# Stacked fp32r scores, slabs and stores dealt out over the rounds, the scan behind the maximum, and ScalarE copying the turned weights of every unit

## What is computed

```python
h = rms_norm(x, g_pre_mix) * (1 + scale_a) + shift_a          # mod = silu(c) @ w_ada + b_ada
q, k, v, xl, yl, ga, gr = split(h @ w_in)
q, k = rope(q, pos), rope(k, pos)
# prompt: blocks of 128 queries against their own and the previous 128 keys
s = (q @ k.T) / 8;  s = where(0 <= d <= 128 and k_pos >= 0, s, -1e30)
m = maximum(max(s), sink);  p = exp(s - m)
o = (p / (sum(p) + exp(sink - m))) @ v
xc = causal_conv4(xl);  r, i = sigmoid(xc @ w_a + b_a), sigmoid(xc @ w_x + b_x)
hl = scan(a = exp(-8 r softplus(-lam)), u = sqrt(1 - a^2) * i * xc)
o_lru = hl * gelu(yl)
merged = sigmoid(ga) * (o @ w_attn) + sigmoid(gr) * (o_lru @ w_lru)
x = x + gate_a * rms_norm(merged @ w_out, g_post_mix)
# then a top-1 group, top-2 expert SwiGLU layer over 32 experts, with its own norms and modulation
```

## Time and profile before

| | us |
|---|---|
| median of 3 runs | 1672.56 (1672.17 to 1677.83) |
| the profiled execution | 1672.81, its span 1671.0 |
| TensorE busy | 1593.2 (95%) |
| VectorE / ScalarE / GpSimd busy | 744.5 / 626.4 / 126.8 |
| granted TensorE clock, mean | 0.981 |
| mean DMA rate | 242 GB/s |

### The profile page before, as it was taken

How to read it: one execution, slowest core, us unless ns; L and a number is a source line. 1 busy time by engine, 2 the same in 40 slices (tenths; PEclk the granted TensorE clock), 3 DMA queues, 4 the chain that set the end, 5 groups by cost and what they waited for, 6 DMA issues and landing times. The chain is left out here.

```text
span 1671.0 us, 27190 instructions
## 1 busy us (share of the span) xinstructions
PE 1593.2 (95%) x11089; PEld 1154.4 (69%) x11089; DVE 744.5 (45%) x1474; ACT 626.4 (37%) x1130; POOL 126.8 (8%) x218
## 2 busy tenths in 40 slices
PE   6999989999999989999999999988998999999997
PEld 2889967888888889999999989752333333333334
DVE  3523467888888764454455456660000000000006
ACT  4535545666666553343544354411110111111113
POOL 0000011111111000000000030000000000000002
PEclk7999999999999999999999999999999999999999
DMA  9464571111111385373447554979999999999988
GB/s 360 168 209 139 171 253 36 55 55 55 55 48 49 124 283 175 126 277 127 159 144 239 189 200 153 350 296 397 421 408 427 425 415 426 409 412 390 407 334 321
DMA packets 98866, 404.66 MB, mean 242 GB/s; under 512 B 13431, under 2 KB 42135, under 8 KB 85800
## 3 DMA queue, kind: packets, MB, share of 16 engines
q1 hardware_dynamic: 88816, 381.28, 59.9%
q0 software_dynamic: 6992, 17.78, 2.7%
q10 hardware_dynamic: 2936, 3.88, 0.8%
HBM read 364.83 MB, written 44.32 MB: 245 GB/s over the span
## 5 line engine op out<-in xcount | busy, mean ns | idle before, releaser
L1234 ACT ACTIVATE wup<-wraw 128x1024 fp32r<-128x1024 f32 x120 | 126.7, 1059 | 265.6 <-PE ps L2113 222.6
L1734 DVE TENSOR_TENSOR wlow<-wraw,wup 128x1024 fp32r<-128x1024 f32 x112 | 136.9, 1224 | 148.6 <-ACT wup L1234 148.0
L2113 PE MATMUL ps<-wg,xT 128*32 128x512 f32 (+2 forms) x1072 | 158.8, 621 | 11.1 <-DMA wg<-w_gate 10.3
L2113 PE MATMUL ps<-wd,aT 128*32 128x512 f32 (+2 forms) x1072 | 150.0, 596 | 6.2 <-DMA wd<-w_down 4.6
L2113 PE MATMUL ps<-wu,xT 128*32 128x512 f32 (+2 forms) x1072 | 148.6, 594 | 2.8 <-DMA wu<-w_up 2.8
L2113 PE MATMUL ps<-h_up,wup 128*128 128x384 f32 (+1 forms) x384 | 125.7, 327 | 3.4 <-DVE wlow L1734 3.4
L2113 PE MATMUL ps<-h_up,wlow 128*128 128x384 f32 (+1 forms) x384 | 124.5, 324 | 0.0
L2113 PE MATMUL ps<-h_low,wup 128*128 128x384 f32 (+1 forms) x384 | 124.5, 324 | 0.0
L2113 PEld LDWEIGHTS ps<-wd,aT 128*32 128x32 f32 (+2 forms) x1072 | 47.3, 117 | 105.6 <-issue 103.9
L2113 PEld LDWEIGHTS ps<-wg,xT 128*32 128x32 f32 (+2 forms) x1072 | 45.0, 120 | 107.5 <-issue 104.2
L2113 PE MATMUL ps<-hp_up,wA_up 128*128 128x352 f32 x312 | 107.6, 345 | 1.1 <-DVE hp_low L1488 1.1
(11 more groups left out here) (416 smaller groups left out, 3227.7 us busy)
## 6 DMA issues: line engine op xcount, KB each, us to landing
wg<-w_gate SPq DMA_DIRECT2D x32, 2048.0 KB
wu<-w_up SPq DMA_DIRECT2D x32, 2048.0 KB, 15.6
wd<-w_down SPq DMA_DIRECT2D x32, 2048.0 KB, 13.7
wraw<-w_ga SPq DMA_DIRECT2D x24, 512.0 KB, 3.7
wraw<-w_gr SPq DMA_DIRECT2D x24, 512.0 KB, 3.8
wraw<-w_at SPq DMA_DIRECT2D x24, 512.0 KB, 3.5
wraw<-w_lr SPq DMA_DIRECT2D x24, 512.0 KB, 3.5
wraw<-w_out SPq DMA_DIRECT2D x24, 512.0 KB, 3.5
```

The source lines that it names most:

```text
L1234: act.activation(wup[n % UP][:, :, :], wraw[n % RAW][:, :, :], ACT.Copy).then_inc(w_rounded, 1)
L1734: V.tensor_tensor(low_part(n)[:, :, :], wraw[n % RAW][:, :, :], wup[n % UP][:, :, :].bitcast(F32), ALU.subtract).then_inc(w_split, 1)
L2113: return pe.matmul(out, lhsT, rhs, start=start, stop=stop, skip_group_check=True)
```

## The change

1. **Scores.** Queries and keys are rounded and split after the rotation (ScalarE `round_query`, VectorE `split_query`, the same for two key tiles), stored to `q_dram` and `k_dram` with the rounded and the rest part above each other on the partitions, and loaded back for each block (`load_keys`: four DMAs of 64 partitions, `load_queries`: two a round). The contraction now holds the two parts of a query in 64 + 64 rows. Four fp32r matmuls a unit (two for each of its two heads) replace two fp32 matmuls. GpSimd has no part in the rounds any more.
2. **Round 0** takes only the second half of the keys in all steps (`c0 = P`), and the mask has no block dimension any more.
3. **Slabs**: one in step 3 of each round, two buffers; bank 1. The second modulation part is finished in round 7. Half outputs move to earlier steps.
4. **Stores**: h is stored in the rounds, one k a round; attention outputs go to a buffer of their own, `oS`, which must be stored before the next round's first output is written.
5. **The scan** stands in step 4 behind `first`, and in that step `conv` stands behind `second`.
6. **ScalarE** copies the turned weights of all units.

In the diff and in the lists below `kst` is the stacked keys and `ps<-ident,pp` a turning.

```diff
-            return (((0, 0),), ((0, 1), (1, 0)), ((1, 1), (2, 0)), ((2, 1),), ((3, 0),), ((3, 1),), ((4, 0), (4, 1)), ((5, 0), (5, 1)),
+            return (((0, 0), (0, 1)), ((1, 0), (1, 1)), ((2, 0), (2, 1)), ((3, 0),), ((3, 1), (4, 0)), ((4, 1),), ((5, 0),), ((5, 1),),
                     ((6, 1), (7, 1), (8, 1)), ((9, 1), (10, 1), (11, 1)))[s]
...
+            def q_store(u):
+
+                sp.wait_ge(kq_split, u + 3)
+                sp.wait_ge(st_kq, kq_stored(u))
+                for part in range(2):
+                    for a in range(2):
+                        sp.dma_start(head_rows(q_dram, part)[:, u, a, :], head_rows(q_part(u, part), a)).then_inc(st_kq, 16)
+
...
+            def load_keys(i):
+
+                if i < BLKS:
+                    ge(sp, u_scores, KC * (i - 1))
+                    c0 = P if i == 0 else 0
+                    for half in range(2):
+                        for a in range(2):
+                            sp.dma_start(head_rows(kst[i % 2], half)[:, a, :, c0:2 * P].bitcast(F32),
+                                         head_rows(k_dram, a)[:, :, (i - 1) * P + c0:(i + 1) * P]).then_inc(ld_kq[i % 2], 16)
...
+            sp.wait_ge(s_dve, 6)
+            sp.wait_ge(st_kq, kq_stored(KC - 1))
+            load_keys(0)
+            load_queries(0)
+            q_store(KC - 1)
+            sp.wait_ge(st_side, 64)
             for p in range(2):
-                sp.dma_start(O["kws"][:, p], kcx[:, p, :, NT:P + NT]).then_inc(st_kws, 16)
...
+                sp.dma_start(O["kws"][:, p], kcx[:, p, :, NT:P + NT]).then_inc(st_side, 16)
+            sp.wait_ge(st_kq, kq_stored(KC))
+            load_queries(1)
+            slab_halves(0)
...
             for i in range(1, KC):
                 lg_weights(i)
+                load_queries(2 * i + 1)
+                load_keys(i + 1)
+                load_queries(2 * i + 2)
+                slab_halves(i)
+                h_store(i - 1)
+                if i + 1 == KC:
+                    h_store(i)
                 o_store(i - 1)
...
-                    if 1 <= s <= KC and s % 2 == 0:
+                    if 1 <= s <= KC:
+                        w = (s - 1) % 2
                         act.wait_ge(u_turned, 8 * i + s - 1 + 3)
                         act.wait_ge(u_pv, 8 * i + s - 1 + 1)
-                        act.activation(pT[:, 1, :, :], ps[:, 6, :].rearrange("p (k q) -> p k q", k=4), ACT.Copy).then_inc(u_kept_a, 1)
+                        act.activation(pT[:, w, :, c0 // P:, :], ps[:, 5 + w, :].rearrange("p (a k q) -> p a k q", a=2, k=2)[:, :, c0 // P:, :],
+                                       ACT.Copy).then_inc((u_kept, u_kept_a)[w], 1)
                     if s >= 2:
                         act.wait_ge(u_pv, 8 * i + s - 2 + 3)
-                        act.activation(oT[:, s - 2, bass.ds(i * P, P)], ps[:, 7, 0:P], ACT.Copy).then_inc(u_out, 1)
+                        if s == 2:
+                            act.wait_ge(st_o, 16 * (i + 1))
+                            act.wait_ge(st_kq, kq_stored(KC))
+                        act.activation(oS[:, s - 2, :], ps[:, 7, 0:P], ACT.Copy).then_inc(u_out, 1)
...
             dve.wait_ge(s_pe, 8)
+            dve.wait_ge(st_kq, kq_stored(KC))
...
+                    if not begin and s == 4:
+                        lru_step(i, "scan")
+                    if 4 < s < KC or begin and s == 4:
                         conv(i, s)
                     if s < KC:
                         second(i, s)
+                    if not begin and s == 4:
+                        conv(i, s)
...
-                    if 1 <= s <= KC and s % 2 == 1:
-                        dve.wait_ge(u_turned, 8 * i + s - 1 + 3)
-                        dve.wait_ge(u_pv, 8 * i + s - 1 + 1)
-                        V.tensor_copy(pT[:, 0, :, :], ps[:, 5, :].rearrange("p (k q) -> p k q", k=4)).then_inc(u_kept, 1)
...
                         for a in range(2):
-                            out = ps[:, 3 + s % 2, a * 2 * P:(a + 1) * 2 * P]
-                            ins = mm(out, qst[:, s % 4, a, :], kT[:, s // 4, bass.ds(i * P, 2 * P)], True, True)
+                            out = ps[:, 3 + s % 2, a * 2 * P + c0:(a + 1) * 2 * P]
+                            for part in range(2):
+                                ins = mm(out, qst[n % 3][:, s % 4, a, :], kst[i % 2][:, a, 2 * (s // 4) + part, c0:], part == 0, part == 1)
                         ins.then_inc(u_scores, 1)
-                    if s < KC:
-                        slab(s) if begin else outs(i, s)
+                    if s < KC and not begin:
+                        outs(i, s)
+                    if s == SLAB_STEP:
+                        slab(i)
```

More of the change, by code:

```diff
@@ L52 @@
 N_SLAB = 2 * KC
+SLAB_STEP = 3
 SB = D // 2 // KC
@@ L534, in lane_part, with k_part, q_part, kq_stored @@
             return ap[NS * lane:NS * (lane + 1), 0:FD].rearrange("r (h c) -> r h c", h=2)
+        def k_part(part):
+            return oT[:, 2 + 2 * part:4 + 2 * part, 0:SEQ]
+        def q_part(u, part):
+            return q_low[:, u, 0:SEQ].bitcast(F32) if part else oT[:, u + 3 if u < 5 else u - 2, 0:SEQ]
+        def kq_stored(units):
+            return 16 * 2 + 64 * units
+        def kq_loaded(i, half):
+            return 96 * (i // 2) + 80 + 16 * half
+        def head_rows(ap, a):
+            return ap[HD * a:HD * a + HD]
         def bc(ap, shape):
@@ L1116, in _ @@
                         round_pair((m + 1) % 2, (m + 1) // 2 + 1)
+                    if g == 1 and m > 2:
+                        round_query(m - 3)
                 swap(m, oT[:, m - 2, :])
+            round_query(KC - 1)
             def store_mod(g):
@@ L1179, in act_round @@
             def act_round(i, first=False):
+                c0 = P if first else 0
                 for s in range(KC + 2):
@@ L2326, in pe_round @@
                         for a in range(2):
-                            for hf in range(2):
+                            for hf in blocks:
                                 q = 2 * a + hf
@@ L2739, in constants @@
     out = np.float32(-1e30)
-    masks = np.zeros((P, BLKS, 2 * P), np.float32)
-    masks[:, :, :P] = np.where(k >= q, 0, out)[:, None, :]
-    masks[:, :, P:] = np.where(k <= q, 0, out)[:, None, :]
-    masks[:, 0, :P] = out
+    masks = np.zeros((P, 2 * P), np.float32)
+    masks[:, :P] = np.where(k >= q, 0, out)
+    masks[:, P:] = np.where(k <= q, 0, out)
     t, j = (m % NT)[:, None], np.arange(P + NT)[None, :]
```

211 lines of the change are left out of this document (112 added, 99 removed).

## The result

The changed kernel takes 1686.64 us (median of 5 runs, 1685.14 to 1689.93) against 1672.56 us: the ratio is 1.008, with a 95% interval of 1.006 to 1.0099. It is slower, by 14 us, and outside the range of 1648 to 1675. Its profiled execution has a span of 1683.3 us, 12.3 more than before.

A forecast was written before the change was run, and what follows sets the result against it. TensorE bounds rounds 1 to 7 with VectorE close behind; the chain from scores to weights bounds round 0. 1672.8 - 8.7 (round 0) - 6.3 (rounds 1 to 7) + 2.0 (hand-over) = 1659.8 us, range 1648 to 1675.

The forecast's parts named there:

- Scores: Score matmuls of each unit: four fp32r matmuls take 0.58 us for 0.97, a gain of 0.39, 3.1 us a round.
- TensorE's work in a round: Rounds 1 to 7: cheaper scores less 3.1 us, one slab plus 1.1, so 43.7 becomes 41.7 us.
- VectorE's chain and the pause: Rounds 1 to 7, steps 4 to 7: VectorE 17.3 us against TensorE 15.8, so TensorE waits about 1.5 for unit 7.
- The wait for the output store: ScalarE's first output copy in a round, after the previous outputs' store: no cost in the sum.
- rival B: Hand-over and rounds 1 to 7: 64-partition transfers at half rate delay the output store; 1677 in full, put at 1668; chance 0.22.
- C: Rounds 1 to 7: the whole burst at 245 GB/s lands late, each round 47.7 us, total 1689; chance 0.12.
- The clock in rounds 1 to 7: TensorE's granted clock: a fall to 1.2 GHz was priced for round 0 only, up to 3 us.
- Round 0: First round, half the keys and one slab: 29.9 us, a gain of 8.7 (5 to 11).
- Hand-over: Stores and key loads between sample attention and round 0: 2 us exposed (0 to 5.3).
- Projections: Query and key projections, 97 us: nine of ten added ScalarE copies and VectorE subtractions stand here, free.

## Why the prediction was wrong

- **Scores: right.** 0.58 us a unit was forecast; the four matmuls of unit 6 of round 4 begin at 429.73 and the projection behind them at 430.31 (timeline of PE, kernel after).

```profile
429.73 0.75 PE L2195 MATMUL ps<-kst,qst 128*128 128x256 f32 x4
430.31 0.33 PE L2195 MATMUL ps<-hp_up,wB_up 128*128 128x352 f32 x1
```

- **TensorE's work in a round: right.** 41.7 forecast, 41.8 measured at full clock.
- **VectorE's chain and the pause: right in size, for a reason that was half wrong.** The chain is 17.0 us (17.3 forecast), and the pause without the wait for the store 1.7 (1.5). But I held the chain against TensorE's work behind the scores of unit 4. The slab in step 7 adds 1.1 us there and leaves the pause as it was. The chain begins with the exponentials of unit 3, and how early these come hangs on the projections ahead of units 1 to 3. By my sum, moving half outputs behind unit 4 would help because TensorE had more to do there; it helps because the chain starts earlier.
- **The wait for the output store: the step that failed.** The forecast gave it no cost and left it to rivals B and C. B's own working was near: a landing "near 19" against a need at 17, from the round's first scores; round 4 in the trace has 18.8 (396.9 to 415.7) against 17.2 in the kernel without the wait (389.6 to 406.8), and the other rounds up to 1.5 later. Two errors followed. The rate of the burst was taken from a row of 128-partition pieces at 350 GB/s, and while the keys move it is 212 to 266. And the price was put at nothing in the sum (at 2 us a round in rival B), where it is 2.4 us a round, 17 us in all: mean rounds of 46.6 against 44.2 without the wait, with two buffers (at full clock 46.3 to 46.4 against 43.3). Rival B at its full half rate ended at 1677 and C at 1689, and the result, 1686.6, lies between them by the mechanism that both share. They got 0.22 and 0.12, and B was set at the middle of its span, although the one fact that would decide it, a transfer of 64 partitions, was in no row and the sentence on the page of the Trainium skill, in rival B, spoke for the slow end.
- **The clock in rounds 1 to 7: not in the sum.** I priced a half-speed clock for round 0 alone. A pause of TensorE of 1.7 to 2.8 us at the end of a round brings it down in most rounds: 0.9 us a round in the kernel with two buffers, 6.4 in all. In the kernel after, rounds at full clock take 46.1 and the seven 46.8 in the mean of the rows above, 0.7 each (some of it round 1's, which is the longer one at full clock too). So a forecast pause has a second price: the rounds of 43.2 should have been 44.1.
- **Round 0: right within its bounds, and about 2.3 us short.** From its first maximum (224.1) to that of round 1 it takes 32.2 us after and 38.6 before, a gain of 6.4 for 8.7 forecast (5 to 11). The granted clock of 0.61 all through is the case that was priced at up to 3 us. In the other kernels here it took 30.5 to 32.3.
- **Hand-over: right, with the term at 2.** From the first turning of sample weights to the copy that opens round 0's first unit it takes 11.8 us after (211.88 to 223.68) and 9.2 before (215.08 to 224.27), 2.6 more, and VectorE waits for the stores of query 7 and of the sample cache, as forecast (timeline of DVE, kernel after).

```profile
218.97 0.49 DVE L1677 COPY oSs<-ps 128x128 f32<-128x128 f32 x2 [4.95 <-DMA q_dram<-q_low]
223.11 0.06 DVE L1686 MEMSET xlp<- 128x3 f32 x1 [3.65 <-DMA kws<-kcx]
```

  That the whole start is level with the forecast (6.3 us gained, 6.7 forecast) is partly luck. The profiled execution reached the samples 3.2 us earlier than that of before, and the kernel with two buffers, whose code is the same up to there, reached them at 214.74, 2.9 us later.
- **Projections: right.** They take 97.0 us of 97 with ten more copies and subtractions beside them, and what lies behind the rounds did not move.

Put together: the kernel with neither of the two missing terms is the one with two buffers and the pause filled, and it takes 1660.35 us where the forecast was 1659.8. That the two meet within 1 us is in part luck: in its profiled execution the rounds 1 to 7 gained 4.8 us on before where 6.3 were forecast, and what lies ahead of round 1 gained 7.9 where 6.7 were. Leaving the pause to the clock adds 9.5 us (1669.9; 6.4 of it stand in the rounds), and the late store 16.7 more (1686.6). So the sum was that of a kernel in which the store is never late and the clock never falls.

## What to carry to other kernels

When a change gives a result a buffer of its own that a store must empty, put the store's landing, not its issue, against the first write into the buffer again, and follow the engine that waits in order: what stands behind that wait (here a table load and one unit's exponentials) is what costs. Two faults in a row may hide part of each other, so mend them together before judging either. And to find where a chain begins, take the last wait in front of it: moving work that lies behind that wait, or filling it with work that covered another, wins nothing.

## What the runs showed of the hardware

- A pause of TensorE of 1.66 us was followed by products at half speed in four of seven rounds, and filling it with products that nobody reads removed that in all of them. In the two kernels whose longest pause in a round was 0.8 us there was no such product in rounds 1 to 7.
- While keys were read, the DMAs moved 212 to 266 GB/s with the keys over 64 partitions and 328 to 332 with them over 128, with as many bytes and transfers; four issues took SyncE 2.55 us (0.64 each) and 2.12.
- The table load ahead of unit 3's exponentials, 1.28 us of ScalarE in every round, begins only when ScalarE gets to it behind the wait (416.00), so it lies in the chain that sets the round's end.
